# A decoder layer on one core: the second layer norm from differences to a pivot, gathered in the last block

## What is computed

```python
def layer_norm(x, g, b):
    mu = xf.mean(-1, keepdims=True)
    var = jnp.square(xf - mu).mean(-1, keepdims=True)
    return ((xf - mu) * lax.rsqrt(var + LN_EPS) * g + b)
...
mix = jnp.einsum('bsd,de->bse', ga * br_a + gb * br_b, w_out)
h = layer_norm(ALPHA * x + mix, ln1_g, ln1_b)
u = jnp.square(jax.nn.relu(jnp.einsum('bsd,df->bsf', h, w_ff1) + b_ff1))
f = jnp.einsum('bsf,fd->bsd', u, w_ff2) + b_ff2
return layer_norm(ALPHA * h + f, ln2_g, ln2_b)
```

## Time and profile before

| | us |
|---|---|
| median of 3 runs | 1890.46 (1890.34 to 1891.09) |
| the profiled execution | 1891.25 |
| its span, first to last instruction | 1889.7 |
| TensorE busy | 1826.7 (97%) |
| VectorE busy | 911.7 (48%) |
| ScalarE busy | 773.2 (41%) |

### The profile page before, as it was taken

One profiled execution on the slowest core, in us unless ns is written; L12 is line 12 of the kernel. 1 busy time (PEld: TensorE's weight loads), 2 busy tenths in 40 slices (PEclk: granted clock), 3 DMA queues, 4 the chain that ended last, 5 costly groups with the idle time before them and its releaser, 6 DMA issues.

```text
span 1889.7 us, 33735 instructions
## 1 busy us (share of the span) xinstructions
PE 1826.7 (97%) x12750; PEld 1766.2 (93%) x12750; DVE 911.7 (48%) x1197; ACT 773.2 (41%) x1063; POOL 103.7 (5%) x208
## 2 busy tenths in 40 slices
PE   7999999999999999999599999999999999999993
PEld 7999999988888889999499999999999999999992
DVE  5555543365555545644664444444444444444444
ACT  5444543455555553332344332443234332343322
POOL 0000000101111111100000000000000000000000
PEclk9999999999999999999799999999999999999996
DMA  8555565676666656655347576666667666666631
GB/s 258 145 155 149 158 176 162 201 271 236 213 211 247 203 200 208 214 170 172 102 159 240 181 239 206 216 207 213 222 199 236 209 216 205 214 211 210 220 102 56
DMA packets 270911, 369.04 MB, mean 195 GB/s; under 512 B 11921, under 2 KB 264529, under 8 KB 267905
## 3 DMA queue, kind: packets, MB, share of 16 engines
q1 hardware_dynamic: 250368, 249.17, 43.5%
q0 software_dynamic: 9088, 106.90, 14.5%
q10 hardware_dynamic: 11392, 12.13, 1.9%
HBM read 356.02 MB, written 70.71 MB: 226 GB/s over the span
## 4 chain that ended last, share of the span: by engine, by line
PE 95%; DVE 3%; ACT 1%; DMA 0%; issue 0%; DVEq 0%; SPq 0%; ACTq 0%
PE psM L960 29%; PE psM L961 29%; PE psM L962 29%; PE psM L1008 1%; PE psO L1055 1%; PE psT L1034 1%; PE psM L1021 1%; PE psO L1068 1%; DVE s_r L885 1%; DVE s_r L894 1%; PE psT L980 0%; PE psO L1070 0%; PE psO L1065 0%; PE psM L1012 0%; PE psT L1149 0%; PE psO L1083 0%
## 5 line engine op out<-in xcount | busy, mean ns | idle before, releaser
L670 DVE TENSOR_TENSOR s_wlo<-s_raw,s_whi 128x1024 fp32r<-128x1024 f32 x468 | 573.7, 1227 | 730.7 <-ACT s_whi L414 725.5
L414 ACT ACTIVATE s_whi<-s_raw 128x1024 fp32r<-128x1024 f32 x468 | 495.1, 1058 | 900.0 <-PE psM L962 876.4
L960 PE MATMUL psM<-s_xhi,s_whi 128*128 128x320 f32 x1248 | 392.2, 314 | 10.6 <-DVE s_xlo L675 9.9
L961 PE MATMUL psM<-s_xlo,s_whi 128*128 128x320 f32 x1248 | 386.7, 310 | 0.0
L962 PE MATMUL psM<-s_xhi,s_wlo 128*128 128x320 f32 x1248 | 386.7, 310 | 0.0
L960 PE MATMUL psM<-s_hhi,s_whi 128*128 128x320 f32 x1024 | 317.8, 310 | 9.0 <-DVE s_hlo L880 8.7
L961 PE MATMUL psM<-s_hlo,s_whi 128*128 128x320 f32 x1024 | 317.5, 310 | 0.0
L962 PE MATMUL psM<-s_hhi,s_wlo 128*128 128x320 f32 x1024 | 317.4, 310 | 0.0
L962 PE MATMUL psM<-s_uhi,s_wlo 128*128 128x320 f32 x1024 | 316.4, 309 | 0.0
L961 PE MATMUL psM<-s_ulo,s_whi 128*128 128x320 f32 x1024 | 316.4, 309 | 0.0
L960 PE MATMUL psM<-s_uhi,s_whi 128*128 128x320 f32 x1024 | 316.4, 309 | 0.0
(11 more groups left out here) (160 smaller groups left out, 1593.0 us busy)
## 6 DMA issues: line engine op xcount, KB each, us to landing
s_raw<-in_w_ff_dram SPq DMA_DIRECT2D x256, 512.0 KB, 3.7
s_raw<-in_w_in_dram SPq DMA_DIRECT2D x156, 512.0 KB, 4.1
s_kvbuf<-in_kT_b_dram POOLq DMA_DIRECT2D x8, 2448.0 KB, 9.1
s_kvbuf<-in_v_b_dram POOLq DMA_DIRECT2D x8, 2304.0 KB, 8.3
s_raw<-in_w_out_dram SPq DMA_DIRECT2D x32, 512.0 KB, 3.5
out_b_s_dram<-in_cache_b_kv_dram POOLq DMA_DIRECT2D x16, 1008.0 KB, 6.1
s_raw<-in_w_branch_a_dram SPq DMA_DIRECT2D x16, 512.0 KB, 3.5
gates_scratch<-s_gstage ACTq DMA_DIRECT2D x16, 320.0 KB, 3.3
```

Of the source, the lines that this page charges most:

```text
L414: act.activation(whi[:, slot], raw[:, slot], ACT.Copy).then_inc(hi_done, 1)
L670: dve.tensor_tensor(wlo[:, slot], raw[:, slot], whi[:, slot].bitcast(F32), ALU.subtract).then_inc(lo_done, 1)
L960: pe.matmul(out, wh, hi[:, t0 + k], start=first and k == 0, stop=False)
L961: pe.matmul(out, wh, lo[:, t0 + k], start=False, stop=False)
```

## The change

The second layer norm is taken apart, and the down half of the last block is written out group by group (g = 0 to 7) in place of the loop.

- **A pivot.** Tiles 0 to 7 are final after group 3. VectorE folds their sum to one row (`folded`), TensorE averages it over the partitions behind the first chunk of group 4, and ScalarE copies twice that to `piv`, which is the mean of tiles 0 to 7. VectorE subtracts it from all 16 tiles in group 4 (`take_pivot`).
- **Early sums.** The differences in tiles 0 to 7 sum to nothing. Those of tiles 8 to 13 are added up in `t1`, and the squares of tiles 0 to 13 in `gt8`, on ScalarE and VectorE, in groups 5 to 7. TensorE averages both over the partitions behind the third chunk of group 7.
- **Behind the last group** only tiles 14 and 15 are new: added, squared and averaged one by one, into the same two PSUM rows. The first holds the mean less the pivot (`delta`), the second the mean square; the variance is the second less `delta` squared.
- **The apply.** VectorE subtracts `delta` and multiplies by the reciprocal root (in PSUM). Of the 16 tiles' gain and bias, ScalarE does 11 and VectorE 5 (`Y_BY`).
- **The stores.** SyncE issues eight, of two tiles each, and it waits for them. GpSimd waits only for its own transfers.

```diff
--- before.py
+++ after.py
@@ -160,6 +163,11 @@
...
+        folded, piv_sum, pivoted, off_pivot = (sem(n) for n in ("folded", "piv_sum", "pivoted", "off_pivot"))
...
+        B3 = 3 * C_BLK + C_FF + 32
+        Y_BY = "AADAAADAAADAAADD"
+        MULS = ((0, 2), (2, 4), (4, 8), (8, 12), (12, 16))
...
+        def sum_group(g):
+            return evac[(g + 1) % 2], 24 + (E_FF + 8 + g % 2) // 2 + g // 2 + 1
@@ -277,6 +302,12 @@
+            yv = o["yT"].rearrange("(t p) n -> p t n", p=P)
+            for k in range(8):
+                sp.wait_ge(*y_ready(2 * k))
+                sp.wait_ge(*y_ready(2 * k + 1))
+                sp.dma_start(yv[:, 2 * k:2 * k + 2], r[:, 2 * k:2 * k + 2]).then_inc(y_out, 16)
+            sp.wait_ge(y_out, 16 * 8)
...
@@ -401,7 +432,6 @@
                         piece += 1
             pool.wait_ge(out_kv, 16 * 12)
             pool.wait_ge(out_cache, 16 * 8 * DB)
-            pool.wait_ge(y_out, 16 * 4)
@@ -622,11 +652,7 @@
-                    if li == 0:
-                        act.activation(hhi[:, 4 * p:4 * p + 4], r[:, 4 * p:4 * p + 4], ACT.Copy).then_inc(h_hi, 1)
-                    else:
-                        act.dma_start(o["yT"].rearrange("(t p) n -> p t n", p=P)[:, 4 * p:4 * p + 4],
-                                      r[:, 4 * p:4 * p + 4]).then_inc(y_out, 16)
+                    act.activation(hhi[:, 4 * p:4 * p + 4], r[:, 4 * p:4 * p + 4], ACT.Copy).then_inc(h_hi, 1)
@@ -654,10 +680,40 @@
-            with act.Fori(0, 7) as q:
+            def square_pair(g):
+                act.wait_ge(*sum_group(g))
+                act.activation({4: xres[:, 0], 5: xres[:, 1], 6: t2[:, 0]}[g], r[:, 2 * g:2 * g + 2], ACT.Square).then_inc(sq_early, 1)
+            for g in range(7):
                 for j in range(4):
-                    split(q + (3 * 16 + C_FF // 4 + 9), j)
-            layer_norm(1, ln2g, ln2b)
+                    split(3 * 16 + C_FF // 4 + 9 + g, j)
+                    if g == 4 and j == 1:
+                        act.wait_ge(piv_sum, 1)
+                        act.activation(piv, psO[:, 0, 0:NTOK], ACT.Copy, scale=2.0).then_inc(pivoted, 1)
+                    if g == 5 and j == 0:
+                        for p in range(2):
+                            act.wait_ge(off_pivot, 3 + p)
+                            act.activation(gt8[:, 4 * p:4 * p + 4], r[:, 4 * p:4 * p + 4], ACT.Square).then_inc(sq_early, 1)
+                        square_pair(4)
+                    if g == 6 and j == 0:
+                        square_pair(5)
+            square_pair(6)
+            act.activation(eps[:, 1:2], eps[:, 0:1], ACT.Sqrt)
+            for t in (14, 15):
+                act.wait_ge(tail_d, t - 13)
+                act.activation(t2[:, 1, t - 14], r[:, t], ACT.Square).then_inc(tail_sq, 1)
+            act.wait_ge(stat_d, 1)
+            act.activation(delta, psO[:, 0, 0:NTOK], ACT.Copy).then_inc(delta_in, 1)
+            act.wait_ge(delta_in, 1)
+            act.activation(dsq, delta, ACT.Square).then_inc(dsq_in, 1)
+            act.wait_ge(var_in, 1)
+            act.activation(std, lnrow[:, 2], ACT.Sqrt, bias=eps[:, 0:1]).then_inc(root_in, 1)
+            for t in range(16):
+                if Y_BY[t] == "A":
+                    act.wait_ge(mul_d, muls_for(t))
+                    act.activation(r[:, t], r[:, t], ACT.Identity, bias=ln2b[:, t:t + 1], scale=ln2g[:, t:t + 1]).then_inc(y_act, 1)
...
@@ -940,12 +993,87 @@
             with dve.Fori(0, 4) as q:
                 up(3, q, 0)
                 up(3, q, 1)
-            with dve.Fori(0, 3) as q:
-                down(3, q, 0)
-                down(3, q, 1)
-            down(3, 3, 0)
-            down(3, 3, 1, last=True)
-            layer_norm(1, ln2g, ln2b)
+            def take_pivot():
+                dve.wait_ge(pivoted, 1)
+                for p in (2, 3, 0, 1):
+                    part = r[:, 4 * p:4 * p + 4]
+                    dve.tensor_tensor(part, part, lnx[:, 0:1].broadcast_to([P, 4, NTOK]), ALU.subtract).then_inc(off_pivot, 1)
+            def sum_squares(step, out, more):
+                dve.tensor_tensor(out, out, more, ALU.add).then_inc(sq_sum, 1)
+                dve.wait_ge(sq_sum, step)
+            for g in range(7):
+                for j in range(4):
+                    split(3 * 16 + C_FF // 4 + 9 + g, j)
+                    if g == 4 and j == 1:
+                        take_pivot()
+                    if g == 5 and j == 2:
+                        dve.wait_ge(sq_early, 2)
+                        sum_squares(1, gt8[:, 0:4], gt8[:, 4:8])
+                        sum_squares(2, gt8[:, 0:2], gt8[:, 2:4])
+                        dve.wait_ge(sq_early, 3)
+                        sum_squares(3, gt8[:, 0:2], xres[:, 0])
+                    if g == 6 and j == 2:
+                        dve.wait_ge(sq_early, 4)
+                        sum_squares(4, gt8[:, 0:2], xres[:, 1])
+                dve.wait_ge(chunk_done, B3 + 4 * g + 4)
+                pair = r[:, 2 * g:2 * g + 2]
+                if g == 4:
+                    dve.wait_ge(off_pivot, 4)
+                dve.tensor_tensor(pair, pair, psM[(g + 1) % 2][:, :, 0:NTOK], ALU.add).then_inc(evac[(g + 1) % 2], 1)
+                if g < 4:
+                    add_sum(pair, sum_group(g), g + 11)
+                    if g == 3:
+                        dve.wait_ge(summed, 14)
+                        dve.tensor_tensor(lnrow[:, 2], lnrow[:, 0], lnrow[:, 1], ALU.add).then_inc(folded, 1)
+                elif g == 5:
+                    dve.wait_ge(*sum_group(5))
+                    dve.tensor_tensor(t1[:], r[:, 8:10], pair, ALU.add).then_inc(d_sum, 1)
+                elif g == 6:
+                    dve.wait_ge(*sum_group(6))
+                    dve.wait_ge(d_sum, 1)
+                    dve.tensor_tensor(t1[:], t1[:], pair, ALU.add).then_inc(d_sum, 1)
+            dve.wait_ge(d_sum, 2)
+            dve.tensor_tensor(lnrow[:, 0], t1[:, 0], t1[:, 1], ALU.add).then_inc(part_sums, 1)
+            dve.wait_ge(sq_early, 5)
+            sum_squares(5, gt8[:, 0:2], t2[:, 0])
+            dve.tensor_tensor(lnrow[:, 1], gt8[:, 0], gt8[:, 1], ALU.add).then_inc(part_sums, 1)
+            dve.wait_ge(chunk_done, B3 + 32)
+            for t in (14, 15):
+                dve.tensor_tensor(r[:, t], r[:, t], psM[0][:, t - 14, 0:NTOK], ALU.add).then_inc(tail_d, 1)
+            shift = psO[:, 0:1, 0:NTOK].broadcast_to([P, 4, NTOK])
+            scale = psT[:, 0:1, 0:NTOK]
+            def less_mean(p):
+                dve.tensor_tensor(r[:, 4 * p:4 * p + 4], r[:, 4 * p:4 * p + 4], shift, ALU.subtract).then_inc(less_d, 1)
+            def affine(t):
+                dve.wait_ge(mul_d, muls_for(t))
+                dve.tensor_scalar(r[:, t], r[:, t], ln2g[:, t:t + 1], ln2b[:, t:t + 1], ALU.mult, ALU.add).then_inc(y_dve, 1)
+            dve.wait_ge(delta_in, 1)
+            less_mean(0)
+            dve.wait_ge(stat_sq, 1)
+            dve.wait_ge(dsq_in, 1)
+            dve.tensor_tensor(lnrow[:, 2], psO[:, 1, 0:NTOK], dsq, ALU.subtract).then_inc(var_in, 1)
+            less_mean(1)
+            dve.wait_ge(root_in, 1)
+            dve.reciprocal(psT[:, 0, 0:NTOK], std).then_inc(rstd_in, 1)
+            dve.wait_ge(rstd_in, 1)
+            for k, (lo, hi) in enumerate(MULS):
+                p = lo // 4
+                if lo >= 8:
+                    less_mean(p)
+                dve.wait_ge(less_d, p + 1)
+                part = r[:, lo:hi]
+                dve.tensor_tensor(part, part, scale.broadcast_to([P, hi - lo, NTOK]), ALU.mult).then_inc(mul_d, 1)
+                for t in range(lo, hi):
+                    if Y_BY[t] == "D":
+                        affine(t)
         @block.tensor
...
@@ -1152,17 +1280,46 @@
-            with pe.Fori(0, 4) as b:
+            def up_groups(b):
...
+            with pe.Fori(0, 3) as b:
+                up_groups(b)
...
-            layer_norm(1)
+            up_groups(3)
+            def row_sum(out, row, start, stop):
+                return pe.matmul(out, onesD[:], row, start=start, stop=stop)
+            mean_d, mean_sq = psO[:, 0, 0:NTOK], psO[:, 1, 0:NTOK]
+            for g in range(8):
+                par = (g + 1) % 2
+                pe.wait_ge(evac[par], 24 + (E_FF + 8 + g % 2) // 2 + g // 2)
+                for j in range(4):
+                    pe.wait_ge(u_lo, 24 + 2 * j + 2)
+                    chunk(B3 + 4 * g + j, j, psM[par], uhi, ulo, 4 * j, j == 0, j == 3)
+                    if g == 4 and j == 0:
+                        pe.wait_ge(folded, 1)
+                        row_sum(mean_d, lnrow[:, 2], True, True).then_inc(piv_sum, 1)
+                    if g == 7 and j == 2:
+                        pe.wait_ge(part_sums, 2)
+                        row_sum(mean_d, lnrow[:, 0], True, False)
+                        row_sum(mean_sq, lnrow[:, 1], True, False)
+            for t in (14, 15):
+                pe.wait_ge(tail_d, t - 13)
```

(33 more changed lines are left out.)

## The result

The kernel after takes **1877.06 us** (median of 4 runs, 1876.89 to 1877.16) against 1890.67 before (median of 4, one run more than in the table above): 13.6 us less, ratio 0.9928 with a 95% interval of 0.9911 to 0.9945. The forecast was 1876.7, in a range of 1873.0 to 1884.8. The profiled execution took 1877.16 us and has a span of 1875.6 us; 1875.9 was forecast.

The account below looks back on a forecast made before the run. TensorE was taken as the bound up to the last block, then a 39.8 us tail; 2.9 (block) + 22.85 (last landing) + 0.3 (end) = 26.05, 13.75 us less: 1876.7 us, range 1873.0 to 1884.8.

Parts of the forecast that it names:

- the DRAIN's cover: End of program: GpSimd no longer waits for stores, so its 7.745 us DRAIN hides under the last block's matmuls; 8.0 us gone.
- block: the stop at the pivot: Last block, group 4: TensorE stands until VectorE has folded group 3's sum, 1.15 us (0.8 to 1.5).
- block: three row sums: Last block: one row sum in group 4 and two in group 7, paid in full on TensorE, 1.75 us.
- end of block to the reciprocal's end: Layer norm's end: from VectorE's first take of row 14 (t = 0), the reciprocal runs from 6.0 to 8.15 us.
- to the last store's issue: Layer norm's end: SyncE issues the last of eight stores at t = 20.15 us.
- to the last landing: Layer norm's end: the last store lands 2.7 us after issue, at t = 22.85 (22.3 to 24.0), where now 31.5.
- to the end: Behind the last landing: SyncE's wait, a 0.007 us DRAIN and closing semaphores, 0.3 us where now there are 8.3.
- The rival built on it: Program's end: the DRAIN waits for something else there and stays last, time 1884.4 us; chance 0.12.
- The tail: Second layer norm behind the last block: rows 14 and 15, reciprocal, apply and stores, last landing at t = 22.85 us.
- The shorter path to the last landing: From VectorE's take of the last matmul's sum to the last store's landing: 8.65 us of the 13.75 gain.
- The 0.58 for one row sum: Last block: price of one fp32 row sum on TensorE, taken as 0.58 us from a span of 0.53 to 0.8.
- The slower rival: Last block written out: its 768 matmuls lose pace to code fetching; at 0.18 us each, time about 1902 us; chance 0.03.

Follow-up runs that it names:

- experiments 1 and 2: Kernel before with SyncE, not GpSimd, waiting for the four stores: 1882.02 us; kernel after with GpSimd also waiting for the eight stores: 1884.90 us.
- experiment 6: Kernel after with the pivot's row sum behind the second chunk of group 4, not the first: 1875.90 us, span 1874.3.
- 10: No pivot at all, on the kernel after with later pivot sum, 14 affines on ScalarE and last two stores swapped: 1873.67 us against 1873.90.
- experiments 3 and 4: Kernel after with GpSimd waiting until ScalarE has done six or nine tiles of the apply: 1877.15 and 1878.91 us, spans 1875.6 and 1877.4.
- a_pool_waits: Kernel after with GpSimd waiting for the eight stores as well as SyncE: 1884.90 us, 7.8 more than the kernel after.
- b_sp_waits: Kernel before with one edit, SyncE instead of GpSimd waits for the four stores: 1882.02 us against 1890.02, ratio 0.9957.
- a_no_pivot: Pivot's row sum, copy and subtractions removed, on the kernel after with 14 affines on ScalarE and last two stores swapped: 1873.67 us against 1873.90.

## Why the prediction was right, step by step

| term | forecast, us | measured, us | by |
|---|---|---|---|
| the DRAIN's cover | −8.0 | −8.0 and −7.8 | experiments 1 and 2; last landing to end 8.25, then 0.41 |
| block: the stop at the pivot | +1.15 | +1.35 | 2.95 less the 1.60 of experiment 6 |
| block: three row sums | +1.75 | +1.60 | 6; 0.53 for one by 10 |
| end of block to the reciprocal's end | 8.15 | 7.7 | timeline after |
| to the last store's issue | 20.15 | 19.8 | 1872.42, SyncE |
| to the last landing | 22.85 | 22.5 | 1875.2 |
| to the end | 0.3 | 0.4 | closing rows |

Of the 1.35 at the pivot, 1.07 is the idle time that the row shows, and 0.16 is the end of the last matmul before it, under which the next would have started. The last 0.1 lies inside the row sum: from its start to the next matmul's are 0.40 (1797.92 to 1798.32), and 0.29 where it has not waited. That next matmul has its successor 0.39 later in both, so this belongs to the price of a row sum and not to the stop. The same place in experiment 6:

```profile
1800.31 0.70 PE L1299 MATMUL psO<-s_lnrow,s_onesD 128*128 128x320 f32 x2
...
1800.60 0.55 PE L1088 MATMUL psM<-s_uhi,s_whi 128*128 128x320 f32 x1
...
1800.99 0.31 PE L1089 MATMUL psM<-s_ulo,s_whi 128*128 128x320 f32 x1
```

- **The DRAIN.** The step rested on one row and on a reason; experiments 3 and 4 now give its law. The rule cited from the Trainium skill (VectorE: DVE Perf Modes, "The DRAIN you can't avoid"), that DRAINs of preamble and postamble are constant at about 12 ns on all engines, is near what SyncE shows (7 ns), and does not hold for GpSimd (7,745 ns in every trace), nor for TensorE (1,568), ScalarE (1,226) and VectorE (841) in the kernel after. The rival built on it, 1884.4, is nearly the time of `a_pool_waits` (1884.90): right price, wrong cause.
- **The tail.** The sum was 0.3 to 0.4 too long. ScalarE's copy of the mean took 0.44, not the 0.53 of the root, and the two row sums of differences 1.34, not 1.55, since the clock stayed at 1.00 until past the last row sum (stretch, each engine's busy us, clock, DMA):

```profile
1854.00:1859.00 5.00, 1.60 (x6) 0.78 (x5) 3.97 (x4) 1.50 (x4) 0.00 (x0) 1.00 0.00 0
```

VectorE's chain of 10.3 us behind the reciprocal was as forecast (1860.38 to 1870.65).
- **Luck in the base.** The shorter path to the last landing was forecast at 8.65 and is 8.98 between the two profiles, but the profile of before held 0.7 of halved clock. Against `b_sp_waits`, whose first row sums ran at full clock, it is 8.3, and 0.4 of that is the smaller last store. The median came out 0.4 above its forecast and the span 0.3 below: the forecast let the profiled execution stand 0.79 above the median, as it did for the kernel before, and for the kernel after it stands only 0.10 above.
- **The block.** The 0.58 for one row sum does not follow from the two rows named for it, which give 0.74 and 0.95, each partly at half clock; it was a choice, and near the measured 0.53. It was right that the row sum stops TensorE for as long as VectorE's folding is late, and that VectorE's other additions are covered.
- **The slower rival.** Written out, the last block's matmuls keep their pace: in `a_no_pivot` the down half of the last block is 1.07 longer than at 0.1467 a matmul, and its two row sums of 0.53 account for that. Nothing is left for the fetching of code.
- **The bounds.** The forecast's terms with their bounds add up to 1875.7 to 1878.9, not to the 1874.8 to 1879.5 that it states. The measured time lies in both.
- **What I had not seen.** 3.2 us lay open in the version as changed: 1.35 at the pivot, 1.4 in the split of the affines, and 0.4 that is put down to the order of two stores. The first and the last could be read from the diff with the trace of before.

## What to carry to other kernels

Look at what each engine does after its last wait: here GpSimd's fixed 7.7 us of closing work stood behind a wait that SyncE could take, and one moved line gave more than half of the whole gain. A reduction put into a stage that is bound by TensorE costs its matmuls in full and, in addition, any lateness of what it reads, so its place in the stream should be one chunk after its operand is ready. When a tail is shortened by deferring work, sum both sides: the path to the reciprocal got 11 us shorter here and the path behind it 2 us longer.

## What the runs showed of the hardware

- GpSimd's DRAIN took 7,745 ns in all twelve profiles, whether it began 92, 9 or 6 us before the last landing was seen, or right behind it, and with stores under way or none.
- The granted clock made the same two row sums 2.06 us in one profile and 1.34 in another, with 1.8 us of idle array ahead of both. In the first it fell to 1.2 GHz while they ran. So one profile of a short tail on TensorE can have 0.7 us of chance in it.
- An fp32 row sum of 320 columns costs 0.53 us in the stream at full clock (experiments 6 and 10), 3.6 of the fp32r matmuls of the same size, 0.147 each.
